# Sequences' attention placed between the projection tiles, in half slots, in one decoder layer step

## The reference

```python
def mixer(xn, ...):                       # prompt and sequences alike
    q, gates, rows, hq, hk, hv, logf, og = split(xn @ w_in)   # the projection
    kc, vc = compress(cached and new rows)                    # short keys, values
    # three attention branches, each softmax(q k + bias) v, gated and added:
    #   compressed: all kc; gives the importance of each 64-token block
    #   selected:   past blocks, the unimportant ones masked
    #   window:     the last 512 rows
    o_att = g0 * o_cmp + g1 * o_slc + g2 * o_win
    o_hg  = gated_linear_recurrence(hq, hk, hv, logf, state)  # chunk by chunk
    return concat(norm(o_att), norm(o_hg) * silu(og)) @ w_out

y = x + 0.5 * ffn1(norm(x))
y = y + mixer(norm(y))
y = y + 0.5 * ffn2(norm(y))
```

## Time and profile before

| | us |
|---|---|
| median of 3 runs | 3188.43 (3187.55 to 3188.77) |
| the profiled execution, its own time | 3181.32 |
| its span | 3179.7 |
| TensorE busy in the span | 2992.5 (94%) |
| mean granted TensorE clock, share of full | 0.935 |

### The profile page before, as it was taken

The page is one execution under the profiler, slowest core; times in us unless marked ns, Lnnn a source line. Parts: engine busy times, 40 slices in busy tenths (PEclk is TensorE's granted clock), DMA queues, the critical chain, the costliest instruction groups (busy, mean ns, idle before and its releaser), DMA issues.

```text
span 3179.7 us, 46641 instructions
## 1 busy us (share of the span) xinstructions
PE 2992.5 (94%) x18952; PEld 2815.2 (89%) x18952; DVE 1450.1 (46%) x1776; ACT 974.3 (31%) x1092; POOL 119.9 (4%) x180
## 2 busy tenths in 40 slices
PE   6999999999999999999994767969999999999999
PEld 3788999999999999999983556649999999999999
DVE  2424445334444444565545434354444433444433
ACT  3423332223222333333323111123343322322322
POOL 0000000000000011100000000121000000000000
PEclk9999999999999999999996655569999999999999
DMA  7364554455554555433214440235454445545444
GB/s 186 101 190 121 149 152 146 139 162 157 150 146 137 148 181 204 147 132 113 107 54 130 137 125 20 65 113 153 139 151 145 137 141 158 159 145 152 131 139 139
DMA packets 675398, 437.43 MB, mean 138 GB/s; under 512 B 29133, under 2 KB 664029, under 8 KB 667741
## 3 DMA queue, kind: packets, MB, share of 16 engines
q1 hardware_dynamic: 661026, 421.29, 44.1%
q0 software_dynamic: 1856, 12.87, 1.1%
q10 hardware_dynamic: 12396, 1.61, 0.5%
HBM read 422.33 MB, written 21.65 MB: 140 GB/s over the span
## 4 chain that ended last, share of the span: by engine, by line
PE 91%; SPq 3%; DVE 2%; issue 1%; ACTq 1%; DMA 1%; POOL 1%; ACT 0%; DVEq 0%; POOLq 0%
PE bank L406 21%; PE bank L407 21%; PE bank L408 21%; PE bank L738 4%; PE bank L740 4%; PE bank L739 4%; PE bank L1266 2%; PE bank L666 2%; PE bank L668 2%; PE bank L667 2%; SPq L1344 1%; PE bank L1105 1%; PE bank L1573 1%; PE bank L1567 1%; SPq L1357 1%
## 5 line engine op out<-in xcount | busy, mean ns | idle before, releaser
L406 PE MATMUL bank<-xh,whi 128*128 128x320 f32 x3072 | 951.4, 310 | 20.1 <-POOL xl L1837 20.1
L407 PE MATMUL bank<-xl,whi 128*128 128x320 f32 x3072 | 950.4, 309 | 0.0
L408 PE MATMUL bank<-xh,wlo 128*128 128x320 f32 x3072 | 950.4, 309 | 0.0
L312 DVE TENSOR_TENSOR wlo<-wraw,whi 128x2048 fp32r<-128x2048 f32 (+1 forms) x321 | 649.8, 2025 | 523.6 <-ACT whi L308 522.7
L308 ACT ACTIVATE whi<-wraw 128x2048 fp32r<-128x2048 f32 (+1 forms) x321 | 543.3, 1693 | 716.9 <-PE bank L408 716.9
L406 PEld LDWEIGHTS bank<-xh,whi 128*128 128x128 f32 x3072 | 578.0, 188 | 21.3 <-POOL xl L1837 21.0
L407 PEld LDWEIGHTS bank<-xl,whi 128*128 128x128 f32 x3072 | 578.0, 188 | 0.2 <-issue 0.2
L408 PEld LDWEIGHTS bank<-xh,wlo 128*128 128x128 f32 x3072 | 577.7, 188 | 0.0
L406 PE MATMUL bank<-hh,whi 128*128 128x320 f32 x1408 | 436.2, 310 | 9.2 <-DVE hl L366 9.2
L407 PE MATMUL bank<-hl,whi 128*128 128x320 f32 x1408 | 435.7, 309 | 0.0
L408 PE MATMUL bank<-hh,wlo 128*128 128x320 f32 x1408 | 435.5, 309 | 0.0
(11 more groups left out here) (308 smaller groups left out, 2568.8 us busy)
## 6 DMA issues: line engine op xcount, KB each, us to landing
wraw<-in_w_ffn_gate_up SPq DMA_DIRECT2D x176, 1024.0 KB, 5.4
wraw<-in_w_ffn_down SPq DMA_DIRECT2D x128, 704.0 KB, 4.5
wraw<-in_w_mix SPq DMA_DIRECT2D x52, 1024.0 KB, 4.8
pages<-in_cache_cmp SPq DMA_DIRECT2D x128, 128.0 KB, 2.1
wraw<-in_w_mix_out SPq DMA_DIRECT2D x16, 1024.0 KB, 5.4
kt_s<-in_slc_k SPq DMA_DIRECT2D x64, 128.0 KB, 2.0
s_v<-in_slc_v SPq DMA_DIRECT2D x64, 128.0 KB
o_win_sample<-in_state_win_kv POOLq DMA_DIRECT2D x8, 1008.0 KB, 15.7
```

Of the source, the lines that this page charges most:

```text
L312: dve.tensor_tensor(wlo[:, a % 2, 0:size], wraw[:, a % RAW, 0:size], whi[:, a % 2, 0:size].bitcast(F32), ALU.subtract).then_inc(s["lo_read ...
L406: pe.matmul(b, whi[:, a % 2, c], h[:, kk, :], start=first, stop=False)
L407: pe.matmul(b, whi[:, a % 2, c], lo_[:, kk, :], start=False, stop=False)
L408: mm = pe.matmul(b, wlo[:, a % 2, c], h[:, kk, :], start=False, stop=end)
```

## The change

Four things are changed.

1. The sequences' attention moves out of its own stage. A tile of the projection is now two half slots of 24 matmuls each; slot number hs = 2 (a - 21) + half for tile a. The 8 units of the prompt use half slots from -2 on, eight half slots for each pair of units, so they lie beside the first 16 recurrence tiles. From half slot 29 (tile 35, second half) the sequences use four half slots each: piece 0 `first`, piece 1 two `turn`s of the sequence before and `group_sums`, piece 2 two more `turn`s and `importance`, piece 3 `values` of the sequence before. The last `values` comes behind tile 52.
2. To make room in memory, `wraw` has two buffers during the projection, not four (the other two hold the sequences' scores and biases), so the load of tile a waits until tile a - 2 is split. The keys of a sequence have one buffer instead of two.
3. SP's loads move into the projection's order: the 48 bias loads behind weight tile 27, keys of the next sequence behind each odd tile from 37 or 39 on, values behind each even tile from 40 on.
4. GpSimd prepares the sequences' queries before the recurrence's masks, and takes the compressed keys no longer from a copy in memory: SP loads them per sequence.

```diff
         def in_matmuls(pe, a, half):
...
-            for k in range(KT):
+            for k in range(KT // 2 * half, KT // 2 * half + KT // 2):
...
+        def half_slot(a, half):
+            return 2 * (a - A_H) + half
...
         def pe_in(pe):
...
-                pe_att(pe, a)
-                in_matmuls(pe, a)
+                for half in range(2):
+                    pe_att(pe, half_slot(a, half))
+                    pe_sample(pe, half_slot(a, half))
+                    in_matmuls(pe, a, half)
+            pe_sample(pe, half_slot(N_IN, 0))
...
         def dve_in(dve, link):
...
-                dve_att(dve, link, a)
+                for half in range(2):
+                    dve_att(dve, link, half_slot(a, half))
+                    dve_sample(dve, link, half_slot(a, half))
...
         def sync_in(sp):
...
-                sp.wait_ge(s["lo_ready"], g + 1)
-                sp.dma_start(wraw[:, g % RAW, 0:size], io["w_mix"][a - 1] if a else io["w_gate"]).then_inc(s[f"raw{g % RAW}"], 16)
+                sp.wait_ge(s["lo_ready"], g + (1 if a < 2 else 3))
+                sp.dma_start(wraw[:, a % 2, 0:size], io["w_mix"][a - 1] if a else io["w_gate"]).then_inc(s[f"raw{g % RAW}"], 16)
...
+                if a == 27:
+                    sync_sample_bias(sp)
...
+                if a >= 39 and a % 2:
+                    b = (a - 37) // 2
+                    sp.wait_ge(s["s_sc"], b + 1)
+                    sync_window_keys(sp, b)
+                    sync_keys(sp, b)
+                if a >= 40 and a % 2 == 0:
+                    sync_values(sp, (a - 40) // 2)
+            sync_values(sp, NB - 1)
...
-        START = [A_H + 7 * (n // 2) + 3 * (n % 2) for n in range(8)]
+        START = [8 * (n // 2) + 3 * (n % 2) - 2 for n in range(8)]
...
+        def exp_step(n):
+            return 2 + UNITS[n][0]
...
+        def sample_piece(hs):
+            return divmod(hs - S0, 4) if 0 <= hs - S0 < 4 * (NB + 1) else (0, 4)
...
+            if piece == 0 and it < NB:
+                first(it)
+            if piece == 1:
+                if it:
+                    turn(it - 1, 0)
+                    turn(it - 1, 1)
+                if it < NB:
+                    group_sums(it)
+            if piece == 2:
+                if it:
+                    turn(it - 1, 2)
+                    turn(it - 1, 3)
+                if it < NB:
+                    importance(it)
+            if piece == 3 and it:
+                values(it - 1)
```

More of the change, by code:

```diff
@@ L1045, in build, with att_steps @@
         ev_parity = lambda n, p: (n + 1 - p) // 2
-        def att_steps(a):
-            return [(n, a - START[n]) for n in range(8) if 0 <= a - START[n] <= 6 + UNITS[n][0]]
+        def att_steps(hs):
+            return [(n, hs - START[n]) for n in range(8) if 0 <= hs - START[n] <= values_step(n)]
+        def exp_step(n):
+            return 2 + UNITS[n][0]
         def turned(n, step):
-            return range(2 * (step - 4), min(2 * (step - 3), 2 * UNITS[n][0] + 3)) if step >= 4 else range(0)
+            k = 2 * (step - exp_step(n) - 2)
+            return range(k, min(k + 2, 2 * UNITS[n][0] + 3)) if k >= 0 else range(0)
         def values_step(n):
-            return 6 + UNITS[n][0]
+            return 6 + 2 * UNITS[n][0]
         def buf(a, n):
@@ L1106, in pe_att_values, with pe_att @@
             mm.then_inc(s["a_pv"], 1)
-        def pe_att(pe, a):
-            for n, step in att_steps(a):
+        def pe_att(pe, hs):
+            for n, step in att_steps(hs):
                 if (n, step) == (0, 0):
@@ L1131, in evict_att, with act_att @@
             copy(pt[0:rr, k, :], bank[5 + q % 2][0:rr, :]).then_inc(s["a_ev" + "ad"[q % 2]], 1)
-        def act_att(act, a):
-            for n, step in att_steps(a):
+        def act_att(act, hs):
+            for n, step in att_steps(hs):
                 for k in turned(n, step):
@@ L1209, in dve_att @@
                         evict_att(dve, n, k, dve.tensor_copy)
-                if step == 3:
+                if step == exp_step(n) + 1:
                     dve_att_probs(dve, link, n)
@@ L1213, in dve_att, with pe_sample, scores @@
                     dve_att_scores(dve, link, n, 2 * step)
[L1216 to L1220, removed]
+        S0 = 29
+        def sample_piece(hs):
+            return divmod(hs - S0, 4) if 0 <= hs - S0 < 4 * (NB + 1) else (0, 4)
+        def pe_sample(pe, hs):
+            it, piece = sample_piece(hs)
+            def scores(o, keys):
                 for g2 in range(2):
-                    mm = pe.matmul(bank[2 + k][64 * g2:64 * g2 + 64, :], qb[:, g2, :], keys(b, k)(g2), start=True, stop=True)
+                    mm = pe.matmul(o[64 * g2:64 * g2 + 64, :], qb[:, g2, :], keys[:, :, g2 * P:(g2 + 1) * P],
+                                   start=True, stop=True)
@@ L1267, in values, with act_sample @@
                 mm.then_inc(s["s_pv"], 1)
[L1269 to L1287, removed]
+            if piece == 0 and it < NB:
[14 more added lines that the diff above has]
+                values(it - 1)
+        def act_sample(act, hs):
+            it, piece = sample_piece(hs)
             def exp(b, k, c0, c1):
@@ L1307, in turned @@
                 act.wait_ge(s["s_pv"], b + 1)
[L1308 to L1322, removed]
+                if b == 0:
+                    act.wait_ge(s["a_pv"], 8)
+                act.activation(pts[:, r * 512:(r + 1) * 512], bank[5 + r % 2][:, :], ACT.Copy).then_inc(s["s_eva"], 1)
+            if piece == 0 and it < NB:
+                act.wait_ge(s["s_cm"], it + 1)
+                exp(it, 2, 1552, 1616).then_inc(s["s_ce"], 1)
+            if piece == 1:
+                if it:
+                    turned(it - 1, 0)
+                if it < NB:
+                    act.wait_ge(s["s_wm"], it + 1)
+                    exp(it, 1, 1032, 1552).then_inc(s["s_e"], 1)
+            if piece == 2 and it:
+                turned(it - 1, 2)
+            if piece == 3 and it < NB:
+                act.wait_ge(s["s_sm"], it + 1)
+                exp(it, 0, 0, 1032).then_inc(s["s_e"], 1)
         def pool_sample(pool):
-            pool.wait_ge(s["a_o"], 8)
-            pool.wait_ge(s["kcs_ld"], 16)
+            pool.wait_ge(s["kv_out"], KV_OUT)
+            pool.wait_ge(s["m_ap"], 12)
             pool.memset(qb[:, :, :], 0.0).then_inc(s["qb_zero"], 1)
```

279 lines of the change are left out of this document (142 added, 137 removed).

## The result

The changed kernel takes 3080.53 us (median of 4 runs, 3079.64 to 3082.26), the kernel before in the same session 3187.99 (4 runs, 3185.59 to 3188.77): a ratio of 0.9664, with a 95% interval of 0.965 to 0.9679. Forecast were 3094 (3079 to 3130), so the direction and the range held, and the gain, 107.5 us, was larger than the 94 of the sum. The profiled execution of the changed kernel took 3079.72 us, 101.6 less than the 3181.32 of the one that the sum was made against.

A forecast was written before the change was run, and what follows sets the result against it. TensorE was taken to bound the projection, SP's queue, `values` and load landings the sequences' stage. -204.2 + 94 + 4 + 7 + 2 + 3 = -94 us on 3181.3 gave 3087, plus 7.1 to the median: 3094 us, range 3079 to 3130.

The forecast's parts named there:

- the 94 of the sum: Whole kernel: time removed, less TensorE's added work, waits and clock dips, gains 94 us on the profiled 3181.3.
- removed: Last projection tile's eviction to the recurrence's first decay: 229.9 us shrink to 25.7, so 204.2 us go.
- eight sequences on TensorE: Projection: sequences' pieces at full-clock prices, 12.5 us each with returns to weights, last `values` free: 94 us added.
- VectorE late at piece 2: Before each sequence's fourth transposes: TensorE waits 0 to 0.7 us for VectorE, 4 us in eight sequences.
- units' waits, tile 22 among them: Prompt's units in half slots: 0.5 us of waiting a unit, and 3 us once at tile 22: 7 us.
- ring of two weight buffers: Projection's weight loads: 5 us to spare in a plain tile; 2 us taken for all loads in that queue.
- clock dips: Projection: two more dips of TensorE's clock, like one seen after a unit's `values` and scores, cost 3 us.
- the rival that half slots are too short on VectorE: Projection: TensorE waits 2 us at two pieces a sequence and one step a unit, 48 us: 3131; chance 0.13.
- The rival: Sequences in the projection: SP's queue bounds again, at 30.5 us a sequence against 26.6: 3125; chance 0.10.
- the rival that would have made the kernel slower: Sequences' part of the projection: TensorE's low clock holds and doubles each sequence's 26.6 us: 3307; chance 0.04.

The follow-up runs named there:

- the run of 16 reads: The changed kernel with SP reading the number of every key and value page a second time, 16 more reads a sequence: 3134.92 us.
- VectorE's new order: The changed kernel with VectorE's copies put first where TensorE waits for them, and unit 0 begun a half slot later: 3074.30 us, ratio 0.9646.

## Why the prediction was right, and where its sizes were off

| term, us | forecast | measured |
|---|---|---|
| removed | -204.2 | -205.0 |
| eight sequences on TensorE | +94 | +88 |
| VectorE late at piece 2 | +4 | 1.6, inside the 88 |
| units' waits, tile 22 among them | +7 | +10.5 |
| ring of two weight buffers | +2 | 0.0 |
| clock dips | +3 | +3.2 |
| not taken apart | 0 | +1.7 |
| sum | -94 | -101.6 |

**Removed.** Right. The gates and the first evictions take 24.9 us (25.7 were forecast), and the recurrence kept its clock.

**Added on TensorE.** The mechanism is right, and the full-clock prices hold between weight tiles. Eight times 11.77 less the last `values` are 88, not 94: the four returns to the weights cost 0.47 us a sequence, not 0.8 (half tiles of 3.62 and 3.69 for 3.52), and `values`, the first and the second piece were each 0.1 to 0.25 cheaper.

**Waits.** At the fourth transposes VectorE and TensorE are 0.15 us apart, as forecast 0.1, and the wait of 0.23 us lies inside its 0 to 0.7; the run with more work for VectorE shows that the margin is nil, so the rival that half slots are too short on VectorE was close. Tile 22 waited 3.4 us, as forecast 3. The units waited 7.1 us elsewhere, not 4: the step that failed is that I counted only exponentials and scaling against two half slots, and not the copy of a unit's last transposes behind a weight tile's split, 1.07 us four times, as the run that moves the copy shows. Ring: tiles 0 to 19 take as long as before (the 0.70 us at tile 19 are 0.68 at tile 0), and behind them no wait of TensorE for weights is named.

**SP.** I had its work at 21 us and its room at 5; they are 22.6, with the 0.6 of waiting for a split, and 3.3. The rival did not come, but less room was left than I thought, and once it was used up the waits cost more than their length.

**Clock.** 0.99 and 1.00 in the windows: the rival that would have made the kernel slower did not come. Dense weights around every piece were my reason against it, and no run takes them apart from the rest; what the low level would do, the runs with more work for SP show on a small scale. The dips have the size that I put into the sum. Two half tiles took 5.17 and 4.97 us for 3.62, and the scores of a unit between the wait of 3.37 us and the second of them took 4.12 us for 2.27 (the same kind of scores at either level, windows):

```profile
1388.99:1393.11 4.12, 4.12 (x13) 3.38 (x12) 3.22 (x4) 0.27 (x1) 0.99 (x5) 0.54 0.72 255
1435.32:1437.59 2.27, 2.27 (x13) 2.01 (x12) 1.99 (x7) 0.00 (x0) 0.00 (x0) 1.00 0.80 314
```

That is 4.7 us, less 1.5 for the one dip that the kernel before had too. The Trainium skill (TensorE: Matmul & The Clock Gate, Part 1) has the slow level as the default that activity releases. With the weights behind a slow `values` the trace of the run of 16 reads agrees: their matmuls begin that half tile at 0.61 us and end it at 0.31. With the fp32 `values` it does not: 11.08 us of a busy TensorE stayed at 0.50.

**The median.** I added 7.1 us for the distance of the profiled execution to the median. The changed kernel's profiled execution lay 0.8 under its own: 6 of the 13.5 us between 3094 and 3080.5 are this, and the other 7.6 the terms of the table.

What stays open: of the 1.7 us not taken apart 0.7 lie ahead of tile 19, and the rest is no more than the rounding and half a us of the units' own returns to the weights; what divides the old stage's remaining 183 us between the clock and its chains; and what makes the clock fall in one place and not in another like it.

## What to carry to other kernels

Work that stalls on its loads in a stage of its own can cost just its matmuls at the full clock when it is cut into pieces between dense tiles; the price is then read from the fastest execution of each piece in the old trace, and the room from the engine that must answer within a half tile. Count for that engine everything that lies behind the tile's own eviction and split, copies of other streams too. A gap that a profile puts down to issue can be a wait for an engine: move the copy and see.

## What the runs showed of the hardware that was not expected

A short wait of TensorE can be followed by a loss larger than itself, through the clock, and the loss was larger where fp32 `values` followed than where weights did. With 8 reads more, 0.83 us of waiting were followed by a `values` of 8.70 us (clock 0.65) for 5.72 and 1.96 us by one of 9.11 (0.62), but 1.02 us by 5.80; with 16, 5.45 us by 11.08 (0.50). In the changed kernel the half tiles behind the waits of 1.67 and 3.37 us took 5.17 and 4.97 us (clock 0.67 and 0.70) for 3.62; behind the four of 1.07 they took 3.62, and behind the seven of 1.27 with more work for VectorE one was slow.

The clock also fell where nothing had waited, each time in the weights behind a unit's `values` and scores: in a tile of the kernel before, which took 8.68 us for 7.14, and in a half tile with VectorE's new order, 5.05 for 3.62 (windows, before and then that run):

```profile
1463.05:1471.73 8.68, 8.68 (x50) 8.67 (x50) 2.19 (x4) 0.00 (x0) 0.00 (x0) 0.80 0.20 83
1436.91:1441.96 5.05, 5.05 (x25) 5.04 (x25) 2.11 (x4) 0.00 (x0) 0.00 (x0) 0.68 0.37 151
```

So these runs do not show that the wait alone is the cause. A second read of a page number costs SP about half a us (0.48 in the batch shown), not the 0.65 between two loads.
